# The mLSTM log weights of a two-block transformer kernel: the selected row added in one float32r product instead of a float32 one

## The chip, the cores and the metric

The kernel runs on one core of one Trainium2 chip. The metric is device time in microseconds of the whole program: the median of 3 runs is 2694.84 us (2694.39 to 2695.25).

## What is computed

The program takes 512 tokens and 256 context tokens of width 1024 through two layers of a first block (mLSTM, a gated spatial unit and a convolution side by side, then a gated feed-forward network) and through a second block with two attention mixers. The change lies in the first block's chunked mLSTM. Cut to what matters, the reference does this for each chunk of 128 tokens, each of 4 heads and both directions:

```python
b = jnp.cumsum(fc, axis=-1)
a = b + m[..., None]
Dlog = b[..., :, None] - b[..., None, :] + ic[..., None, :]
Dlog = jnp.where(order, Dlog, -jnp.inf)
m_t = jnp.maximum(a, jnp.max(Dlog, axis=-1))
s = jnp.einsum('bhtk,bhsk->bhts', qc, kc) * jnp.exp(Dlog - m_t[..., None])
```

In the kernel a weight is exp(mask[s, t] + (b - m_t)[t] + (ic - b)[s]). The term in s is a bias per partition of the exponential. The mask and the term in t, the **row** of a head, are what TensorE adds up in PSUM. There are 12 such chunk steps in layer 0 (6 chunks, 2 directions) and 8 in layer 1 (4 chunks, 2 directions), each for 4 heads.

## The kernel before, in words

Everything is written out by hand, engine by engine, with semaphores. Activations lie feature-major. A weight tile of 1024x128 is loaded by SP into a ring of four buffers, split by POOL (`split_weights`, L420 to L427) into an upper part and a rest of type float32r, and multiplied on TensorE as three float32r products (upper times upper, upper times rest, rest times upper). A float32 quantity keeps its accuracy this way with operands of the shorter type. POOL may split tile s when tile s-2 has been used; it waits there on a tiny instruction (L420) for TensorE. In the input projection of the first block the three products are L1508, L1509 and L1510, elsewhere L433, L434 and L436. A tile is 768 columns wide in layer 0 (a pass of 512 and one of 256), and 512 in most of layer 1.

`in_projection` writes TensorE's order by hand. Halves of the projection's tiles 2 to 17 alternate with small pieces of the mLSTM's preparation:

- DVE makes five rows of 8 partitions (4 heads of each direction) over all 768 tokens: `ri` (L2459) is b - m_t. They lie in the memory of `tho`, which is written only later. `columns` (L1467 to L1473) turns two of them, `rb` and `rf`, and the products of `VD` into columns; then DVE copies the identity into `selh` (L2476), an 8 x 8 x 128 selector in float32, computes the arguments `KD` (L2477, L2478) and signals `s_colv`, for which ScalarE's exponentials L1988 and L1989 wait.
- `log_weights(l, i)` (L1476 to L1497) fills one PSUM bank for step i: L1492 is a float32r product, 128 partitions deep and 512 columns wide, of the identity `identr` with the mask; L1495 then adds, for each head, the product of `selh` (8 partitions deep) with 128 columns of `ri`. It uses banks 3 and 4 in turn and waits for ScalarE to have read the bank two steps back (`s_e`).
- ScalarE's `weights(i)` (L1949 to L1960) waits for `s_w` and takes the exponential of the bank, head by head, in 4 instructions (L1959).

The calls of `log_weights` stand behind tile 14 (two), in the middle of tile 15 (two) and behind it (two), in tile 16 (one behind the sums over channels of the convolution, L1503), behind it (two), in tile 17 (one, behind L1503 again) and behind it (two). In layer 1 the last four are empty. After `in_projection` the recurrence begins with `scores` (L1665, which waits for all weights of the layer) in layer 0 and with `update` (L1697) in both.

DVE's further work in this stretch is the convolution (L2311), in portions between its other tasks; in layer 0 it also reads modulation columns (L2269), for which it waits for TensorE (L1391).

Of the kernel before, what the change touches and what calls it, by code (L numbers as in the profile page):

```python
# [14 lines left out]
FP32 = mybir.dt.float32  # L15
FP32R = mybir.dt.float32r
ALU = mybir.AluOpType
# [3 lines left out]
P = 128  # L21
# [3 lines left out]
T = SEQ + CTX  # L25
# [40 lines left out]
def part_start(l, p):  # L66

    return l * LAYER_TILES + N_IN + KT + sum(2 * PARTS[q][1] + KT for q in range(p))
# [40 lines left out]
def mlstm_steps(l):  # L109

    order = ([4, 5, 0, 1, 2, 3], [5, 4, 3, 2, 1, 0])
    return [(d, order[d][i], i == 0, l == 0 or order[d][i] < NX) for i in range(NJ) for d in range(2)] if l < DEPTH else []


def outputs_before(l, t):

    return sum(s[3] for m in range(l) for s in mlstm_steps(m)) + sum(s[3] for s in mlstm_steps(l)[:t])
# [73 lines left out]
def build_program(nc, xT, cT, cb_d, pc_d, fin_d, srow_d, consts_d, sguw_d, wg_d, wmod_d, win_d, wout_d, wgu_d, wdn_d,  # L191
                  b2_d, bmask_d, p_d, wa_d, wao_d, pleg_d, plep_d, wbk_d, wbqz_d, wbo_d, out_d):
    cursor = [nc.sbuf_base + (-nc.sbuf_base) % 64]
    addr_of = {}

    def place(name, shape, dt=FP32, addr=None):
        size = 4
        for s in shape[1:]:
            size *= s
        if addr is None:  # L200
            addr = cursor[0]
            cursor[0] += size + (-size) % 32
        assert addr + size <= nc.sbuf_usable_end, (name, addr + size, nc.sbuf_usable_end)
        addr_of[name] = addr
        return nc.alloc_sbuf_tensor_at(name, shape, dt, offset=addr)

    stack = ExitStack()
    with stack:
# [9 lines left out]
        ident = place("ident", [P, P])  # L218
# [31 lines left out]
        wgl = place("wgl", [P, KT, 16], FP32R)  # L250
        gt = place("gt", [P, NJ, 2, 2, HEADS])
        lf = place("lf", [P, 3, NJ, 8])
        gcol = place("gcol", [P, NJ, 8])
        btm = place("btm", [P, NJ, 8])
        bst = place("bst", [P, NJ, 6])
# [5 lines left out]
        tho = place("tho", [P, HEADS, T])  # L261
# [27 lines left out]

        ri, rf, rb, rm = (place(f"row{i}", [8, T], addr=addr_of["tho"] + i * T * 4) for i in range(4))  # L290
        r2 = place("row4", [8, T], addr=addr_of["vtm"])
        selh = place("selh", [8, 8, P], addr=addr_of["tho"] + 2 * T * 4)
        NUM = [place(f"NUM{e}", [P, HEADS, P + 1], addr=addr_of["YC"] + e * 4 * (HEADS * (P + 1) + 4)) for e in range(2)]
        XF = place("XF", [P, KT, T], addr=addr_of["XH"])
        EP = [place(f"EP{i}", [P, HEADS, P], addr=addr_of["X"] + i * 4 * HEADS * P) for i in range(2 * NJ)]
# [3 lines left out]
        PS = stack.enter_context(nc.psum_tensor("PS", [P, 8, 512], FP32))  # L299
# [114 lines left out]
        def split_weights(pool, s, dyn=0, k=KT):  # L414

            pool.wait_ge(s_raw[s % RING], 16 * (s // RING + 1) + 4 * dyn)
            if s >= 2:
                pool.wait_ge(s_tile, s - 1 + dyn)

            pool.tensor_tensor(word[:, 0:1], ones[:, 0:1], ones[:, 0:1], ALU.mult)  # L420
            for half in range(2):
                ks = slice(half * k // 2, (half + 1) * k // 2)
                src = raw[s % RING][:, 0:k * P].rearrange("p (k c) -> p k c", c=P)[:, ks, :]
                hi, lo = w_hi[s % 2][:, ks, :], w_lo[s % RING][:, ks, :]
                pool.tensor_scalar(hi, src, 1.0, 0.0, ALU.mult, ALU.add).then_inc(s_hi, 1)  # L425
                pool.wait_ge(s_hi, 2 * s + half + 1 + 2 * dyn)
                pool.tensor_tensor(lo, src, hi.bitcast(FP32), ALU.subtract).then_inc(s_split, 1)  # L427
# [894 lines left out]
        @block.gpsimd  # L1322
        def _(pool):
            pool.memset(ones[:], 1.0).then_inc(s_one, 1)
            pool.memset(eps_c[:, 0:1], EPS).then_inc(s_one, 1)
            pool.memset(eps_c[:, 1:2], LN_EPS).then_inc(s_one, 1)
            pool.wait_ge(s_one, 3)
            pool.wait_ge(s_id, 16)
            pool.tensor_scalar(identr[:], ident[:], 1.0, 0.0, ALU.mult, ALU.add).then_inc(s_one, 1)

            for l in range(DEPTH):
                n0 = l * LAYER_TILES
                for n in range(N_IN):
                    split_weights(pool, n0 + n)
                    if l == 0 and n == 3:
                        pool.wait_ge(s_const, 16 * 4)
                        pool.tensor_scalar(mskr[:], mskd[:], 1.0, 0.0, ALU.mult, ALU.add).then_inc(s_one, 1)
                with pool.Fori(0, 2) as i:
                    for u in range(4):
                        split_weights(pool, n0 + N_IN + u, 4 * i)  # L1340
                for p, (h0, hn) in enumerate(PARTS):
                    s = part_start(l, p)
                    with pool.Fori(0, 2 * hn // 4) as i:
                        for u in range(4):
                            split_weights(pool, s + u, 4 * i)
                    with pool.Fori(0, 2) as i:
                        for u in range(4):
                            split_weights(pool, s + 2 * hn + u, 4 * i, hn)
            second_pool(pool)
# [3 lines left out]
        def _(pe):  # L1353
# [121 lines left out]
            def log_weights(l, i):  # L1475

                steps = [s for s in mlstm_steps(l) if s[3]]
                if i >= len(steps):
                    return
                d, j = steps[i][0:2]  # L1480
                o = outputs_before(l, 0) + i
                bank = 3 + i % 2
                if i < 2:
                    pe.wait_ge(s_one, 5)
                    pe.wait_ge(s_mod, 2)
                    pe.wait_ge(s_cole, l + 1)
                    pe.wait_ge(s_mixu, 2 * (l + 1))
                else:
                    pe.wait_ge(s_e, o - 1)
                if i == 0 and l:  # L1490
                    pe.wait_ge(s_tile, l * LAYER_TILES + Q_P)
                pe.matmul(PS[:, bank, :].rearrange("p (h t) -> p h t", h=HEADS), identr[:], mskr[:, d:d + 1, :].to_broadcast([P, HEADS, P]),  # L1492
                          start=True, stop=False)
                for h in range(HEADS):
                    last = pe.matmul(PS[:, bank, h * P:(h + 1) * P], selh[:, 4 * d + h, :], ri[:, j * P:(j + 1) * P],  # L1495
                                     start=False, stop=h == HEADS - 1)
                last.then_inc(s_w, 1)  # L1497

# [56 lines left out]
            def in_projection(l):  # L1555
# [65 lines left out]
                second_half(l, 14)  # L1621
                v_transposed(l, 3)
                log_weights(l, 0)
                log_weights(l, 1)
                first_half(l, 15)
                log_weights(l, 2)
                log_weights(l, 3)
                second_half(l, 15)
# [562 lines left out]
        def _(dve):  # L2191
            links = [0]

            def link(ins):

                links[0] += 1
                ins.then_inc(s_dch, 1)
                dve.wait_ge(s_dch, links[0])
# [15 lines left out]
            def col(l, name, i=0):  # L2214
                return pc[:, l, PC[name] + i:PC[name] + i + 1]
# [132 lines left out]
            for l in range(DEPTH):  # L2348
# [17 lines left out]
                last = dve.tensor_scalar(bcol[:, K_T:V_T], bcol[:, K_T:V_T], K_SCALE, None, ALU.mult)  # L2366
# [56 lines left out]
                for d in range(2):  # L2423
                    last = dve.tensor_scalar(lfv[:, 1, :, d, :], gt[:, :, d, 1, :], 0.0, None, ALU.min)
                link(last)
                link(dve.tensor_tensor(lf[:, 2], lf[:, 1], lf[:, 0], ALU.subtract))
                for d in range(2):
                    last = dve.tensor_copy(lfv[:, 1, :, d, :], gt[:, :, d, 0, :])
# [11 lines left out]
                for r, xs, xc in ((ri, PS[0:8, 3, :], PS[0:8, 4, 0:CTX]), (rf, PS[0:8, 5, :], PS[0:8, 4, CTX:2 * CTX]),  # L2440
                                  (rb, PS[0:8, 6, :], PS[0:8, 7, 0:CTX])):
                    dve.tensor_copy(r[:, ss], xs)
                    last = dve.tensor_copy(r[:, cs], xc)
# [29 lines left out]
                gelu(0)  # L2473
                gelu(1)
                dve.wait_ge(s_cols, l + 1)
                dve.tensor_copy(selh[:], ident[0:8, 0:8].rearrange("p (r c) -> p r c", c=1).to_broadcast([8, 8, P]))  # L2476
                dve.tensor_tensor(KD[:, 0].rearrange("p j e -> p (j e)"), PS[:, 3, 0:8 * NJ], gcol[:].rearrange("p j e -> p (j e)"), ALU.add)  # L2477
                dve.tensor_copy(KD[:, 1].rearrange("p j e -> p (j e)"), PS[:, 3, 8 * NJ:16 * NJ]).then_inc(s_colv, 1)  # L2478
                convolve(l, w, cuts[3], cuts[4])
# [2 lines left out]
                for j in range(nj):  # L2482
                    last = dve.bn_stats(bst[:, j, :], SVT[:, j, :])
                link(last)
                for j in range(nj):
                    last = dve.bn_aggr(bmv[:, j, :], bst[:, j, :])
                last.then_inc(s_svv, 1)
                dve.wait_ge(s_svr, l + 1)
                for j in range(nj):
                    last = dve.tensor_scalar(SVT[:, j, :], SVT[:, j, :], bmv[:, j, 0:1], bmv[:, j, 1:2], ALU.subtract, ALU.mult)  # L2490
                link(last)
                for i in range(2):
                    row = srow[:, 256 * i:256 * (i + 1)].rearrange("p (a c) -> p a c", a=1).to_broadcast([P, nj, 256])
                    last = dve.tensor_tensor(SVT[:, 0:nj, :], SVT[:, 0:nj, :], row, (ALU.mult, ALU.add)[i])
# [16 lines left out]
                for f in range(2):  # L2511
                    last = dve.tensor_tensor(AC[:, f, 0:w], AC[:, f, 0:w], MU[:, 0:w], ALU.subtract)
# [3 lines left out]
                for f in range(2):  # L2516
                    last = dve.scalar_tensor_tensor(out=AC[:, f, 0:w], in0=AC[:, f, 0:w], scalar=col(l, "cg", f), in1=MU[:, 0:w],
                                                    op0=ALU.mult, op1=ALU.mult)
                link(last)
                for f in range(2):  # L2520
                    last = dve.tensor_scalar(AC[:, f, 0:w], AC[:, f, 0:w], col(l, "clb", f), None, ALU.add)
# [269 lines left out]
```

## Time and profile before

| | |
|---|---|
| median of 3 runs | 2694.84 us |
| lowest and highest | 2694.39, 2695.25 us |
| span of the profiled execution | 2693.6 us |
| busy, share of the span | PE 96%, PE weight load 79%, POOL 59%, DVE 52%, ACT 28% |
| data moved | 255.57 MB, mean 95 GB/s |
| chain that ended last | PE 42%, POOL 30%, issue 19%, DVE 5% |

The profiled execution's own time is known by its span, 2693.6 us from the first to the last instruction; the median of the runs is 1.2 us above it. PE is TensorE's matmul side, PEld its weight load, DVE VectorE, ACT ScalarE, POOL GpSimd. PE's busy time is modelled and its matmuls are pipelined, so the start of one to the start of the next tells more than durations do. A float32 product shows as two records of each side, a float32r product as one. The page also gives TensorE's granted clock, as a share of full speed.

### The profile page before, as it was taken

The page shows a single profiled execution, that of the slowest core. Times are in us where ns is not written, and L with a number is a line of the kernel's source. Part 1 is how long each engine was busy: PE and PEld are TensorE (multiplying, and loading weights), DVE is VectorE, ACT ScalarE, POOL GpSimd, SP SyncE. Part 2 cuts the span into 40 slices and gives each one's busy share as a digit, 9 for nine tenths or more (in the row PEclk, how much of TensorE's full clock was granted, in tenths as well). Part 3 has the DMA queues.
Part 4 walks back from the last instruction along what each step waited for, and adds up shares of the span by engine and source line. Part 5 has one row for each costly group of instructions (what it writes and reads, how often), then busy time and mean ns, then how long its engine had stood idle before and what let it go on. Part 6 is the DMA issues. An engine that isn't in the chain of part 4 may idle for free.

```text
span 2693.6 us, 39857 instructions
## 1 busy us (share of the span) xinstructions
PE 2576.0 (96%) x14674; PEld 2116.4 (79%) x14674; DVE 1391.5 (52%) x2054; ACT 754.3 (28%) x1566; POOL 1583.7 (59%) x1668
## 2 busy tenths in 40 slices
PE   5999989999999999999899999999999999899998
PEld 4878978888888886878687877778878887677776
DVE  4862555662662858715533333354454445636744
ACT  3223353211111123234421212222222223324413
POOL 2532224675775665434587777776676765665464
PEclk9999999999999999999999999999999999999999
DMA  6341131332232322111133332433333332222221
GB/s 238 118 156 34 38 152 52 121 123 94 95 126 94 120 86 74 55 50 53 63 95 93 93 94 86 130 106 102 94 95 94 102 102 71 87 89 83 79 94 63
DMA packets 79263, 255.57 MB, mean 95 GB/s; under 512 B 9872, under 2 KB 13712, under 8 KB 78864
## 3 DMA queue, kind: packets, MB, share of 16 engines
q1 hardware_dynamic: 61280, 210.59, 24.3%
q10 hardware_dynamic: 17840, 43.03, 5.3%
q8 instruction: 95, 1.56, 0.2%
q14 instruction: 48, 0.39, 0.1%
HBM read 236.28 MB, written 2.10 MB: 88 GB/s over the span
## 4 chain that ended last, share of the span: by engine, by line
PE 42%; POOL 30%; issue 19%; DVE 5%; DMA 1%; ACT 1%; POOLq 1%; SPq 0%; DVEq 0%; ACTq 0%
POOL w_lo L427 17%; POOL w_hi L425 10%; PE PS L433 8%; PE PS L436 8%; PE PS L434 8%; PE PS L1508 4%; PE PS L1510 4%; PE PS L1509 4%; POOL word L420 2%; PE PS L1495 1%; DVE Z L2230 1%; PE PS L1382 1%; DMA modt<-in_wmod 1%; PE PS L1697 1%; DVE XL L2237 1%
## 5 line engine op out<-in xcount | busy, mean ns | idle before, releaser
L427 POOL TENSOR_TENSOR w_lo<-raw,w_hi 128x512 fp32r<-128x512 f32 (+1 forms) x662 | 957.3, 1446 | 55.2
L433 PE MATMUL PS<-XH,w_hi 128*128 128x512 f32 x2168 | 822.1, 379 | 32.6 <-DVE XL L2595 8.1
L434 PE MATMUL PS<-XL,w_hi 128*128 128x512 f32 x2168 | 794.0, 374 | 0.0
L436 PE MATMUL PS<-XH,w_lo 128*128 128x512 f32 x2168 | 745.0, 375 | 0.0
L420 POOL TENSOR_TENSOR word<-ones 128x1 f32<-128x1 f32 x331 | 103.2, 312 | 1040.4 <-PE PS L436 671.3
L425 POOL TENSOR_SCALAR w_hi<-raw 128x512 fp32r<-128x512 f32 (+1 forms) x662 | 533.4, 806 | 0.0
L433 PEld LDWEIGHTS PS<-XH,w_hi 128*128 128x128 f32 x2168 | 411.4, 190 | 140.9 <-issue 15.1
L434 PEld LDWEIGHTS PS<-XL,w_hi 128*128 128x128 f32 x2168 | 411.6, 190 | 74.1
L436 PEld LDWEIGHTS PS<-XH,w_lo 128*128 128x128 f32 x2168 | 381.4, 190 | 59.4
L1508 PE MATMUL PS<-XH,w_hi 128*128 128x512 f32 (+1 forms) x640 | 235.9, 369 | 10.6 <-DVE XL L2237 10.6
L1509 PE MATMUL PS<-XL,w_hi 128*128 128x512 f32 (+1 forms) x640 | 228.8, 357 | 0.0
L1510 PE MATMUL PS<-XH,w_lo 128*128 128x512 f32 (+1 forms) x640 | 228.7, 357 | 0.0
L2319 DVE TENSOR_TENSOR X<-X,Z 128x768 f32 (+3 forms) x60 | 87.8, 1464 | 226.3 <-ACT Z L1873 221.2
L433 PE MATMUL PS<-HH,w_hi 128*128 128x512 f32 (+1 forms) x528 | 188.4, 357 | 3.4 <-DVE HL L2662 3.4
L434 PE MATMUL PS<-HL,w_hi 128*128 128x512 f32 (+1 forms) x528 | 180.5, 357 | 0.0
L2283 DVE CUSTOM_DVE_ANT_0 cprod<-modv,cb 128x1024 f32<-128x1024 f32 x96 | 165.0, 1719 | 21.2 <-DMA modv<-in_wmod 18.1
L2657 DVE SCALAR_TENSOR_TENSOR Z<-TH,Z 128x768 f32<-128x768 f32 (+1 forms) x44 | 51.4, 1169 | 211.2 <-ACT Z L1854 209.2
L436 PE MATMUL PS<-HH,w_lo 128*128 128x512 f32 (+1 forms) x528 | 159.7, 356 | 0.0
L1508 PEld LDWEIGHTS PS<-XH,w_hi 128*128 128x128 f32 x640 | 125.1, 196 | 31.3 <-issue 11.1
L852 ACT ACTIVATE Z<-PS 128x512 f32<-128x512 f32 x99 | 58.9, 596 | 296.2 <-PE PS L436 292.5
L1510 PEld LDWEIGHTS PS<-XH,w_lo 128*128 128x128 f32 x640 | 124.5, 195 | 17.9
L1509 PEld LDWEIGHTS PS<-XL,w_hi 128*128 128x128 f32 x640 | 125.1, 195 | 15.9 <-issue 0.2
(329 smaller groups left out, 3230.6 us busy)
## 6 DMA issues: line engine op xcount, KB each, us to landing
raw<-in_wgu SPq DMA_DIRECT2D x88, 512.0 KB, 3.5
raw<-in_wa SPq DMA_DIRECT2D x80, 512.0 KB, 3.5
modt<-in_wmod SPq DMA_DIRECT2D x48, 512.0 KB, 9.8
raw<-in_win SPq DMA_DIRECT2D x48, 512.0 KB, 3.6
modv<-in_wmod ACTq DMA_DIRECT2D x48, 512.0 KB, 5.1
raw<-in_wdn SPq DMA_DIRECT2D x32, 512.0 KB, 3.5
QS<-Z ACTq DMA_DIRECT2D x100, 128.0 KB, 2.5
raw<-in_wout SPq DMA_DIRECT2D x16, 512.0 KB, 3.5
```

The source lines that it names most:

```text
L420: pool.tensor_tensor(word[:, 0:1], ones[:, 0:1], ones[:, 0:1], ALU.mult)
L425: pool.tensor_scalar(hi, src, 1.0, 0.0, ALU.mult, ALU.add).then_inc(s_hi, 1)
L427: pool.tensor_tensor(lo, src, hi.bitcast(FP32), ALU.subtract).then_inc(s_split, 1)
L433: pe.matmul(acc(s)[:, a:b], hi, rh[:, i, a:b], start=i == 0, stop=False)
L434: pe.matmul(acc(s)[:, a:b], hi, rl[:, i, a:b], start=False, stop=False)
L436: last = pe.matmul(acc(s)[:, a:b], lo, rh[:, i, a:b], start=False, stop=i == k - 1)
L852: return act.activation(Z[:, n % 4, 0:SEQ], acc(n)[:, 0:SEQ], ACT.Identity)
L1508: pe.matmul(out, hi, XH[:, i, a:b], start=first, stop=False)
L1509: pe.matmul(out, hi, XL[:, i, a:b], start=False, stop=False)
L1510: return pe.matmul(out, lo, XH[:, i, a:b], start=False, stop=i == KT - 1)
L2283: last = dve.tensor_tensor_reduce(out=cprod[:], in0=modv[slots + u][:], in1=cb[:, n, :], scale=0.5, scalar=0.0, op0=ALU.mult, op1=ALU.add, ...
L2319: dve.tensor_tensor(x, x, Z[:, s % 4, 0:w], ALU.add).then_inc(s_used, 1)
```

## The change

The selector `selh` and the float32 product go. In their place stand a float32r operand `RP` of 128 partitions and 768 columns, whose partitions 0 to 7 hold the upper parts of `ri` and whose partitions 32 to 39 hold the rests, the others zero, and a matrix `pick` of 128 x 8 with ones at partitions e and 32 + e of column e. The weights of the product for head e are column e of `pick`, read 128 times with stride zero, so that one product adds upper part and rest of row e to all 128 rows of the output. `pick` is made once by POOL, `RP` once per layer by three DVE instructions where `selh` was copied; it lies where `rf` lay, whose last reader (`columns`) is done by then.

```diff
+        pick = place("pick", [P, 8], FP32R)
...
-        selh = place("selh", [8, 8, P], addr=addr_of["tho"] + 2 * T * 4)
+        RP = place("RP", [P, T], FP32R, addr=addr_of["tho"] + T * 4)
...
             pool.tensor_scalar(identr[:], ident[:], 1.0, 0.0, ALU.mult, ALU.add).then_inc(s_one, 1)
+            pool.tensor_tensor(pick[:], ident[:, 0:8], ident[:, 32:40], ALU.add)
...
                 for h in range(HEADS):
-                    last = pe.matmul(PS[:, bank, h * P:(h + 1) * P], selh[:, 4 * d + h, :], ri[:, j * P:(j + 1) * P],
+                    e = 4 * d + h
+                    last = pe.matmul(PS[:, bank, h * P:(h + 1) * P], pick[:, e:e + 1].to_broadcast([P, P]), RP[:, j * P:(j + 1) * P],
                                      start=False, stop=h == HEADS - 1)
...
                 dve.wait_ge(s_cols, l + 1)
-                dve.tensor_copy(selh[:], ident[0:8, 0:8].rearrange("p (r c) -> p r c", c=1).to_broadcast([8, 8, P]))
+                link(dve.memset(RP[:].bitcast(FP32), 0.0))
+                link(dve.tensor_copy(RP[0:8, :], ri[:]))
+                dve.tensor_tensor(RP[32:40, :], ri[:], RP[0:8, :].bitcast(FP32), ALU.subtract)
                 dve.tensor_tensor(KD[:, 0].rearrange("p j e -> p (j e)"), PS[:, 3, 0:8 * NJ], gcol[:].rearrange("p j e -> p (j e)"), ALU.add)
                 dve.tensor_copy(KD[:, 1].rearrange("p j e -> p (j e)"), PS[:, 3, 8 * NJ:16 * NJ]).then_inc(s_colv, 1)
```

`link` makes DVE wait for the instruction just issued. Every wait, every semaphore and the order of all other work are as before.

VectorE before, in layer 0, where the selector is made (`selh`, `RP`: the operands of the product; `KD`: the arguments of ScalarE's exponentials; `row_180`: `ri`; the first rows are the gated spatial unit's activation, the last the convolution):

```order
L2405 TENSOR_SCALAR Z<-GT 128x768
L2476 COPY selh<-ident 8x1024
L2477 TENSOR_TENSOR KD<-PS,gcol 128x48
L2478 COPY KD<-PS 128x48
L2311 SCALAR_TENSOR_TENSOR AC<-YC,pc,AC 128x8x59
```

and after the change:

```order
L2408 TENSOR_SCALAR Z<-GT 128x768
L2479 MEMSET RP 128x768
L2480 CAST RP<-row_180 8x768
L2481 TENSOR_TENSOR RP<-row_180,RP 8x768
L2482 TENSOR_TENSOR KD<-PS,gcol 128x48
L2483 COPY KD<-PS 128x48
L2314 SCALAR_TENSOR_TENSOR AC<-YC,pc,AC 128x8x59
```

Two instructions more stand ahead of `KD` and of the next portion of the convolution; nothing has moved otherwise.

TensorE before, in layer 0, in the middle of tile 15, where two calls of `log_weights` stand between the tile's pass of 512 columns and its pass of 256:

```order
L1510 MATMUL PS<-XH,w_lo_58 128x512
L1492 MATMUL PS<-mskr,identr 128x512
L1495 MATMUL PS<-row_179,selh 128x128 x4
L1492 MATMUL PS<-mskr,identr 128x512
L1495 MATMUL PS<-row_179,selh 128x128 x4
L1508 MATMUL PS<-XH,w_hi_54 128x256
```

and after the change:

```order
L1513 MATMUL PS<-XH,w_lo_58 128x512
L1494 MATMUL PS<-mskr,identr 128x512
L1498 MATMUL PS<-RP,pick 128x128 x4
L1494 MATMUL PS<-mskr,identr 128x512
L1498 MATMUL PS<-RP,pick 128x128 x4
L1511 MATMUL PS<-XH,w_hi_54 128x256
```

The four products of a call stand in the same place, with other operands.

## Rows read from the trace of the kernel before

**Rows 1.** The page, part 1: busy us, share of the span, instructions

```profile
PE 2576.0 (96%) x14674; PEld 2116.4 (79%) x14674; DVE 1391.5 (52%) x2054; ACT 754.3 (28%) x1566; POOL 1583.7 (59%) x1668
```

**Rows 2.** The chain of waits from 217 to 271 us, by line

```profile
by line: PE PS L1495 24.4%; PE PS L1508 21.3%; PE PS L1510 18.0%; PE PS L1509 17.9%; PE PS L1503 9.6%; PE PS L1492 7.0%; ACT EP L1959 1.2%; PE PS L1398 0.6%; issue 0.5%
```

**Rows 3.** Waits from 1203 us to the end: us in total, times, longest

```profile
POOL word L420 <- PE PS L436: 420.2, 167, 24.3
```

**Rows 4.** TensorE's timeline at tile 15 of layer 0: start us, us

```profile
225.01 0.40 PE L1508 MATMUL PS<-XH,w_hi 128*128 128x512 f32 x1
...
225.71 0.40 PE L1492 MATMUL PS<-mskr,identr 128*128 128x512 f32 x1
226.03 1.15 PE L1495 MATMUL PS<-row,selh 8*128 8x128 f32 x8
227.12 0.51 PE L1492 MATMUL PS<-mskr,identr 128*128 128x512 f32 x1
227.55 1.15 PE L1495 MATMUL PS<-row,selh 8*128 8x128 f32 x8
228.64 0.39 PE L1508 MATMUL PS<-XH,w_hi 128*128 128x256 f32 x1
```

**Rows 5.** The line L1495 alone: ns of one min/median/max, first and last start

```profile
L1495 PE MATMUL PS<-row,selh x160: 270/270/372, 217.4 to 1202.3; 8*128 8x128 f32 x160
```

**Rows 6.** TensorE's timeline after a pair of calls: passes of 256, of 512

```profile
229.09 0.41 PE L1508 MATMUL PS<-XH,w_hi 128*128 128x256 f32 x1
...
229.73 0.41 PE L1508 MATMUL PS<-XH,w_hi 128*128 128x256 f32 x1
...
232.75 0.28 PE L1508 MATMUL PS<-XH,w_hi 128*128 128x256 f32 x1
...
233.10 0.39 PE L1492 MATMUL PS<-mskr,identr 128*128 128x512 f32 x1
...
237.53 0.63 PE L1508 MATMUL PS<-XH,w_hi 128*128 128x512 f32 x1
...
238.81 0.63 PE L1508 MATMUL PS<-XH,w_hi 128*128 128x512 f32 x1
```

**Rows 7.** Stretches: length, busy us (x count) of PE, PEld, DVE, ACT, POOL, granted clock, DMA

```profile
228.50:233.00 4.50, 4.50 (x26) 4.38 (x26) 0.00 (x0) 1.15 (x4) 0.00 (x0) 0.62 0.00 0
...
1184.00:1189.00 5.00, 5.00 (x19) 4.06 (x19) 0.00 (x0) 1.71 (x7) 0.00 (x0) 0.66 0.00 0
283.00:289.00 6.00, 6.00 (x52) 5.91 (x51) 3.22 (x9) 1.28 (x4) 0.00 (x0) 1.00 0.00 0
269.00:278.00 9.00, 7.77 (x43) 7.38 (x43) 4.88 (x6) 5.86 (x17) 3.52 (x3) 0.62 0.14 56
```

**Rows 8.** TensorE's timeline in the recurrence, at 283 us

```profile
283.33 1.05 PE L1697 MATMUL PS<-vtm,Ks 128*128 128x129 f32 x8
```

**Rows 9.** ScalarE's and TensorE's timeline at the end of layer 0's log weights

```profile
267.53 0.69 ACT L1908 ACTIVATE qfm<-PS,bcol 128x512 f32<-128x512 f32 x1 [0.36 <-PE PS L1510]
...
268.76 1.14 ACT L1959 ACTIVATE EP<-PS,gcol 128x128 f32<-128x128 f32 x4 [0.18 <-PE PS L1495]
...
270.34 1.14 ACT L1959 ACTIVATE EP<-PS,gcol 128x128 f32<-128x128 f32 x4 [0.43 <-PE PS L1495]
...
271.54 0.79 PE L1665 MATMUL PS<-qfm,kfm 128*128 128x128 f32 x2 [1.23 <-ACT EP L1959]
```

**Rows 10.** VectorE's selector, its nearest rows, who waits for it, and its idle time

```profile
L2476 DVE COPY selh<-ident x2: 674/678/682, 124.2 to 1105.8; 8x1024 f32<-8x1024 f32 x2
L2637 DVE MEMSET SS<- 128x768 f32 x1 | 0.7, 698 | 0.2 <-DVE cb L2260 0.2
L2461 DVE TENSOR_TENSOR row<-row,mprev x2: 945/946/946, 107.2 to 1094.5; 8x768 f32<-8x768 f32 x2
L1988 ACT ACTIVATE KD<-KD x2: 273/278/282, 131.8 to 1111.6; 128x96 f32<-128x96 f32 x2
DVE bst L2483 <- ACT SVT L1931: 7.4, 1, 7.4
```

## The prediction

> **What bounds the kernel now.** I read the page first: TensorE is busy 96% of the span, no other engine above 59% [rows 1]. A share over the whole span does not say who ends last where the change works, so next comes the chain of waits over 217 to 271 us, the stretch of layer 0 that holds its twelve calls of `log_weights`. It runs on TensorE but for 1.2% on ScalarE; the float32 product L1495 alone is 24.4% of it, the mask's product L1492 7.0% [rows 2]. What these lines give up, the stretch gives up.
>
> Does it reach the end? Behind 1203 us POOL, which splits all weights and stands on the chain as well, waits for TensorE before 167 tiles, 420 us in all [rows 3]. It is paced by TensorE, its loads with it, and the other waits are between neighbours too. A microsecond saved on TensorE moves all that follows.
>
> **What a call costs.** The starts on TensorE's timeline tell it [rows 4]: two calls begin at 225.71 and the next pass at 228.64, so a pair takes 2.93 us, 2.93 to 3.01 in the seven pairs that a pass follows; I take 2.96, or **1.48 us a call**. The mask's product holds 0.41 to 0.43 of it until the first float32 product starts; eight records follow. The line alone has 160 records for 80 products, so each float32 product is two passes [rows 5]. The last lasts 0.37 us, so the eight start (1.15 - 0.37) / 7 = 0.11 us apart: 0.22 a product, and some 0.2 pass before the next kind of product starts.
>
> **What a call will cost.** A float32r product of 512 columns holds TensorE for (225.71 - 225.01) / 3 = 0.233 us [rows 4], one of 256 columns for (233.10 - 232.75) / 3 = 0.117 [rows 6]. None of 128 columns is in the trace. Bounds: by columns, a quarter of 0.233, 0.058; as the two passes of a float32 product of the same shape, 0.22. I take **0.11**: the float32 passes of 128 columns come at this spacing and those of 256 hardly slower, so the weight load of 128 columns seems to set the floor. The two kinds now agree, so the 0.2 us at the change of kind goes. A call is 0.233 + 4 x 0.11 = 0.67, 0.81 less. **20 calls x 0.81 = 16.2 us.** With 0.058 it would be 4.2 more, with 0.22 8.8 less.
>
> The Trainium skill ("TensorE: Matmul & The Clock Gate", Back-to-back issue gap) gives about 81 ns a product for a stream of weight load and 128 columns. The sum by it would be 80 x 0.029 = 2.3 us better, an estimate; the rows here never go below 0.11.
>
> **What ScalarE keeps of it.** In layer 0 the last three calls feed exponentials that stand close together: ScalarE's idle time ahead of the query tile, of step 10 and of step 11 is 0.36 + 0.18 + 0.43 = 0.97 us [rows 9]. TensorE's recurrence starts at 271.54, released by the last of them, after 1.23 us of idle. So these three calls give 0.97 and not 2.4: **1.4 us lost**, and TensorE will wait there some 2.6 us. In layer 1 no call follows the second sum over channels, and ScalarE keeps its distance.
>
> **The clock.** The windows show what the lines cannot. Right behind a pair of calls the granted clock falls from 2.4 to 1.2 GHz: between 228.5 and 233 us its mean is 0.62, between 1184 and 1189 0.66, with TensorE never idle [rows 7]. There are five such stretches, three in layer 0 and two in layer 1, each with 1.70 to 1.71 us of clock missing, (1 - 0.62) x 4.5, or 3.4 us at half speed. What else drops it here is idle time. The pairs are unlike their surroundings in one thing: for 2.2 of 3 us only 8 of the 128 rows of the array work. In the recurrence float32 passes of 128 rows stand 24 in a row and just as close, eight in 1.05 us [rows 8], and the clock stays at 1.00 from 283 to 289 us [rows 7]. So it is the shallow products, I reason, and not float32 or 128 columns that let it fall. The new ones are 128 rows deep and a pair takes 1.35 us. I expect all five stretches to go. At half speed a pass of 256 takes (229.73 - 229.09) / 3 = 0.213 us and one of 512 (238.81 - 237.53) / 3 = 0.427, against 0.117 and 0.233 [rows 4, 6]: 45% of 3.4 us comes back, **5 x 1.55 = 7.8 us**.
>
> **What is added.** DVE zeroes `RP` (0.70 us, by the fill of the same size), then copies and subtracts on 8 x 768 elements (at most 0.95 each, by the nearest row), where it copied the selector in 0.68: 1.9 us more per layer [rows 10]. Behind them on DVE stand the arguments `KD`, two instructions of 0.2 us or less, and the convolution. The selector starts at 124.2 and 1105.8 us, ScalarE takes `KD` at 131.8 and 1111.6 [rows 10]: some 6.7 and 4.9 us of cover, of which 1.9 are used. The convolution is covered by DVE's later waits, 7.4 us for ScalarE in layer 1 [rows 10] and more in layer 0. Cost 0; without that cover, 3.8 us. POOL's sum for `pick` is 8 columns at the program's start, before its first weights have landed: 0.
>
> **The sum.** 16.2 - 1.4 + 7.8 = 22.6 us less. The profiled execution's span of 2693.6 would become 2671.0; from the median of 2694.84, which is 1.2 above it, I get **2672.2 us**.
>
> **Rivals.**
>
> *The clock stays as it is.* The five stretches follow pairs of calls, but not every pair (there is none behind 217 and 1189 us), so the depth of the products may not be what counts; most rows of `RP` are zeros, too. Then the gain is 16.2 - 1.4 = 14.8: 2680.0. Beside it stands a rule of the Trainium skill ("TensorE: Matmul & The Clock Gate", The HAM clock gate): the clock follows how busy TensorE has been, and idle time lowers it. By that rule products issued without a gap should not lower it, and changing their depth should give nothing. Rows 7 speak against it: busy throughout, and half clock. Chance 0.15.
>
> *A sixth stretch goes as well.* From 269 to 278 us the clock is 0.62 over 9 us [rows 7], behind the last pair and the wait for ScalarE. Up to (1 - 0.62) x 9 = 3.4 us would come back: 2669. Against it, the wait grows to 2.6 us. Chance 0.12.
>
> *Narrow float32r is no faster than float32.* At 0.22 a product a call takes 1.11, and 20 save 7.4; ScalarE keeps little of that, the clock gives 7.8: 2680. The same number to a few us covers the change not doing what it says, where the product would be built from two passes. For it: no row has 128 columns. Against it: 256 columns take half of 512, no more. Chance 0.06.
>
> *The saving is caught.* DVE's 3.8 us land on the chain, or a wait behind the stretch absorbs most of it: 2685 to 2690. Rows 3 speak against it. Chance 0.03.
>
> *Slower: weights read with stride zero load slowly.* No weight load in the trace reads one element 128 times. If that cannot stream, each product waits for its weights. It decides from (1.48 - 0.233) / 4 = 0.31 us a product, where a call costs what it did. At 0.43, the slowest spacing of rows 6, a call is 1.95, 20 cost 9.4 more, and the clock is not mended by an array that waits: 2704. Chance 0.02.
>
> **How the numbers follow.** The forecast has 0.62 and is the time predicted. The cases at 2669, 2672 and 2680 hold 0.95 of the chance; the unknown spacing adds 4 below. For 8 in 10 the range reaches from 2667 to 2681. A measurement of this kernel tells about 0.2%, 5.4 us, from no change. Faster by more than that are all cases but the slow one and part of the caught one: 0.96; within it 0.02; slower 0.02.
>
> **What would show it.** L1498 as 80 records, not 160, about 0.11 us apart; pairs of calls of 1.35 us; clock 1.00 over tiles 15 to 17 in both layers, save behind the wait at the recurrence's start; that wait at 2 to 3 us; ScalarE's exponentials of `KD` where they were relative to their tile. It is wrong if pairs take over 2 us, if a stretch of half clock is left inside the tiles, or if `RP` shows up in anybody's wait.

## The result, and the profile after

The changed kernel takes **2661.38 us**, the median of four runs (2659.81 to 2666.65). The kernel before, run on the same chip in turn with it, takes 2695.05 (2694.39 to 2696.39). The measured ratio is 0.9888, with a 95% interval of 0.9877 to 0.9900, which is 30 us; the two medians are 33.7 us apart. The changed kernel is faster by 1.1%, and by more than forecast: 2672.2 had been predicted with a range from 2667 to 2681, and the measured median lies below it. The profiled execution of the changed kernel took 2666.65 us, with a span of 2664.4.

The page of the changed kernel, part 1 (answers to [rows 1]):

```profile
PE 2543.3 (95%) x14594; PEld 2097.1 (79%) x14594; DVE 1401.5 (53%) x2058; ACT 751.6 (28%) x1566; POOL 1579.1 (59%) x1669
```

TensorE has 80 records fewer on each side, VectorE four more, POOL one more: this is the change and nothing else. TensorE is busy 33 us less. VectorE's 10 us more do not repeat: it is busy 1392.1 and 1393.6 us in the two further profiles of this kernel (e1, e10), and what was added to it is 2 x (0.70 + 0.55 + 0.95 - 0.68) = 3.0 us.

The product's line alone in the changed kernel (answers to [rows 5]), with what the engine waited for ahead of it:

```profile
L1498 PEld LDWEIGHTS PS<-RP,pick x80: 187/190/192, 215.4 to 1171.1; 128*128 128x128 f32 x80
L1498 PE MATMUL PS<-RP,pick x80: 219/274/277, 215.7 to 1171.1; 128*128 128x128 f32 x80
its engine sat idle before it (us, times) until:
  issue: 0.2, 1
```

There are 80 records, not 160, and the weight load of stride zero takes 187 to 192 ns: it does stream.

TensorE's timeline of the changed kernel at the same places (answers to [rows 4, 9]): start us, us, and in brackets the idle time ahead.

```profile
215.36 0.48 PE L1494 MATMUL PS<-mskr,identr 128*128 128x512 f32 x1
...
222.39 0.40 PE L1494 MATMUL PS<-mskr,identr 128*128 128x512 f32 x1
222.62 0.56 PE L1498 MATMUL PS<-RP,pick 128*128 128x128 f32 x4
223.01 0.44 PE L1494 MATMUL PS<-mskr,identr 128*128 128x512 f32 x1
223.30 0.56 PE L1498 MATMUL PS<-RP,pick 128*128 128x128 f32 x4
223.69 0.33 PE L1511 MATMUL PS<-XH,w_hi 128*128 128x256 f32 x1
...
256.51 0.38 PE L1668 MATMUL PS<-qfm,kfm 128*128 128x128 f32 x1 [2.11 <-ACT EP L1962]
```

A pair of calls goes from 222.39 to 223.69: 1.30 us, **0.65 a call**, where it was 1.48. Four products take 223.01 - 222.62 = 0.39, or 0.098 each in the mean; in the trace the second starts 0.06 us behind the first and each further one 0.11 behind the one ahead. The wait for ScalarE at the recurrence's start is 2.11 us, where it was 1.23.

Stretches of the changed kernel (answers to [rows 7], the columns are the same: length, busy us of PE, PEld, DVE, ACT, POOL, granted clock, DMA):

```profile
215.00:256.00 41.00, 39.40 (x226) 33.26 (x224) 6.14 (x8) 23.33 (x63) 14.75 (x18) 1.00 0.17 52
256.00:267.00 11.00, 10.40 (x65) 9.16 (x66) 6.47 (x12) 4.20 (x11) 2.65 (x3) 1.00 0.01 1
1150.00:1190.00 40.00, 37.83 (x189) 30.22 (x188) 8.58 (x13) 23.80 (x60) 18.62 (x24) 1.00 0.19 55
```

The clock is 1.00 (2.4 GHz) from the first call to the last, in both layers, and stays there in the recurrence behind them. The same in the kernel before:

```profile
217.00:271.00 54.00, 53.30 (x271) 42.39 (x269) 8.23 (x8) 24.28 (x62) 14.88 (x18) 0.90 0.13 39
271.00:284.00 13.00, 12.46 (x63) 11.41 (x64) 5.58 (x11) 4.29 (x11) 1.52 (x2) 0.77 0.01 2
...
1205.00:1212.00 7.00, 5.06 (x19) 3.14 (x17) 1.91 (x3) 5.43 (x9) 2.26 (x3) 1.00 0.10 21
1212.00:1217.00 5.00, 4.68 (x18) 4.16 (x19) 3.71 (x5) 2.25 (x6) 3.36 (x3) 0.66 0.19 75
```

Where the time went is best seen by cutting TensorE's timeline at the same instructions in every kernel. "Calls 0" goes from the first mask product of layer 0 to the first scores of the recurrence (before: 217.02 to 271.54), "start 0" from there to the second group of `update` that follows (283.33); "calls 1" from the first mask product of layer 1 to the first `update` (1174.45 to 1212.32), "start 1" on to the second group (1217.59). The table has all executions profiled, those of the experiments too; the last column is the measured ratio to the kernel before.

| kernel | calls 0 | start 0 | calls 1 | start 1 | sum | ratio |
|---|---|---|---|---|---|---|
| before | 54.51 | 11.79 | 37.87 | 5.27 | 109.4 | |
| e6_before, the same | 54.49 | 12.06 | 39.29 | 3.77 | 109.6 | 0.9991 |
| e5_dve | 54.47 | 12.09 | 39.32 | 3.75 | 109.6 | 0.9987 |
| e2_shift | 51.42 | 12.06 | 37.81 | 5.36 | 106.7 | 0.9997 |
| **the change** | 41.15 | 9.59 | 28.02 | 3.77 | 82.5 | 0.9888 |
| e1_again, the same | 41.16 | 9.57 | 28.02 | 3.77 | 82.5 | 0.9905 |
| e10_change, the same | 41.15 | 9.60 | 28.02 | 3.76 | 82.5 | 0.9902 |
| e3_deep32 | 45.44 | 9.59 | 31.57 | 3.76 | 90.4 | 0.9923 |
| e4_40deep | 44.19 | 12.12 | 30.71 | 3.77 | 90.8 | 0.9914 |
| e7_shallow_r | 53.88 | 10.72 | 37.35 | 5.36 | 107.3 | 0.9986 |
| e8_last3old | 42.40 | 11.20 | 28.02 | 5.32 | 86.9 | 0.9908 |
| e9_early | 40.63 | 11.75 | 28.02 | 3.77 | 84.2 | 0.9893 |

The change is worth 109.4 - 82.5 = **26.9 us** in these four pieces, and that repeats to 0.1 us in three executions of it. The rest of the difference between two runs lies elsewhere and does not repeat: the two profiles of the kernel before differ by 4.6 us in span and by 0.2 in these pieces. Between the first profiles of the two kernels this rest is 1.7 us ahead of calls 0, 4.3 between start 0 and calls 1, and 3.7 the other way behind start 1. The stretch between start 0 and calls 1 takes 891.1 us before and 886.8 in the change, but also 887.7 in e2 and 886.7 in e7, whose products are 8 rows deep; so it is not the change that shortens it.

### The profile page after: what moved, and what is told of

It is laid out like the page before. It is cut to its first block, busy times and chain, and to the rows that moved or that the text cites. A ratio compares the mean times of both kernels' runs of the same rounds, so it can differ in the third digit from the quotient of the medians.

```text
span 2664.4 us, 39702 instructions
## 1 busy us (share of the span) xinstructions
PE 2543.3 (95%) x14594; PEld 2097.1 (79%) x14594; DVE 1401.5 (53%) x2058; ACT 751.6 (28%) x1566; POOL 1579.1 (59%) x1669
## 4 chain that ended last, share of the span: by engine, by line
PE 42%; POOL 30%; issue 19%; DVE 4%; ACT 1%; DMA 1%; POOLq 1%; SPq 1%; DVEq 0%; ACTq 0%
POOL w_lo L428 17%; POOL w_hi L426 10%; PE PS L434 8%; PE PS L437 8%; PE PS L435 8%; PE PS L1511 4%; PE PS L1512 4%; PE PS L1513 4%; POOL word L421 2%; PE PS L1384 1%; DVE XL L2240 1%; DMA modt<-in_wmod 1%; PE PS L1700 1%; DVE X L1166 1%; DVE Z L2233 1%
## 5 line engine op out<-in xcount | busy, mean ns | idle before, releaser
L2322 DVE TENSOR_TENSOR X<-X,Z 128x768 f32 (+3 forms) x60 | 86.9, 1449 | 223.8 <-ACT Z L1876 218.6
```

The lines of the kernel that those rows point to most:

```text
L2322: dve.tensor_tensor(x, x, Z[:, s % 4, 0:w], ALU.add).then_inc(s_used, 1)
```

## The experiments

**e1_again: the change once more**, in five rounds.

> The change once more, for its interval and a second profile. The first profile shows the stretches of the log weights 22.6 us shorter, as forecast, and the program 29 us shorter (its runs 28 to 35). Theory 'chance downstream': what is beyond 22.6 (the start, one stretch of half clock each behind the recurrence's start, 410, 510 and 2592 us, 6 us lost in mixer B) differs from profile to profile, and the time spreads over several us. Theory 'fixed': the second profile shows the same list and 2659 to 2663 us. Both: 2660 to 2666 us.

Measured: 2663.42 us (2660.64 to 2664.71), before 2690.36 (2686.44 to 2695.12, 15 runs), ratio 0.9905 [0.989, 0.992]. The pieces are those of the first profile. The gain is real and near 26 us; a part of the first 33.7 was the kernel before, which ran 4.7 us quicker here. Outside the pieces the half clock lies where it lay in the first profile up to 2263 us and elsewhere behind that; in e10, a third profile, it differs in more places. So neither theory holds alone: some of these stretches stay where they are and some move.

**e2_shift: the kernel before with the 32 bytes of `pick` taken from the memory**, nothing else.

```diff
+        pick = place("pick", [P, 8], FP32R)
```

> The kernel before with 32 bytes per partition reserved where pick lies, so that all later buffers move as in the change, and nothing else. Theory 'addresses': the slow drift of the gain outside the changed stretches (some 4 us over 1700 us) comes from where buffers lie: 2689 to 2692. Rival: addresses cost nothing: 2694 to 2696.

Measured: 2687.41 us, ratio 0.9997 [0.9988, 1.0006]. What lies behind `pick` in the memory moves by 32 bytes, and that is worth nothing; both times expected were too high, since the kernel before took 2690.36 in this comparison. This execution has 3.1 us less in calls 0 all the same: its clock stayed up behind the calls in tile 15, where it fell in the three other profiles with the calls of the kernel before (before, e5, e6). This execution, then the kernel before:

```profile
227.00:234.00 7.00, 7.00 (x51) 6.15 (x52) 0.00 (x0) 4.10 (x14) 2.63 (x4) 1.00 0.21 72
```

```profile
227.00:234.00 7.00, 7.00 (x41) 6.27 (x40) 0.00 (x0) 2.91 (x10) 0.59 (x2) 0.76 0.00 0
```

So not every pair drops the clock every time. One execution does not tell whether chance or the shift decided it here.

**e3_deep32: 128 rows deep, but float32.**

```diff
-        pick = place("pick", [P, 8], FP32R)
+        pick = place("pick", [P, 8])
...
-        RP = place("RP", [P, T], FP32R, addr=addr_of["tho"] + T * 4)
+        RP = place("RP", [P, T], addr=addr_of["tho"] + T * 4)
...
```

> The change with RP and pick in float32: products 128 rows deep, but in two passes, so a call takes about 1.48 us as before. Theory 'depth': the five stretches of half clock inside the tiles are gone though nothing is quicker: 7.8 us less than before, and with the two at the recurrences' starts 11: 2684 to 2687, with 160 records 0.11 us apart. Rival 'float32 or small products lower the clock': the stretches stay and the time is 2693 to 2696.

Measured: 2667.73 us, ratio 0.9923 [0.9909, 0.9936]. TensorE's timeline of it, and its windows:

```profile
215.52 0.48 PE L1494 MATMUL PS<-mskr,identr 128*128 128x512 f32 x1
215.83 1.05 PE L1498 MATMUL PS<-RP,pick 128*128 128x128 f32 x8
216.64 0.48 PE L1494 MATMUL PS<-mskr,identr 128*128 128x512 f32 x1
216.96 1.05 PE L1498 MATMUL PS<-RP,pick 128*128 128x128 f32 x8
217.77 0.48 PE L1511 MATMUL PS<-XH,w_hi 128*128 128x512 f32 x1
```

```profile
215.00:250.00 35.00, 35.00 (x213) 30.54 (x212) 2.14 (x4) 17.46 (x46) 11.75 (x15) 1.00 0.15 46
261.00:272.00 11.00, 10.91 (x70) 9.67 (x71) 6.01 (x14) 4.01 (x11) 1.82 (x2) 1.00 0.01 2
```

The clock held at 1.00, as expected. The time missed the expectation by some 17 us, because a call takes 1.12 us and not 1.48. The same eight float32 records stand between the same float32r products; what has changed is their depth, and that the weights are read with stride zero, which e7 also has. So the 0.36 us that go belong to the depth, and the change of kind costs nothing that shows: the last record is followed by the next kind after 0.03 us, where it was 0.20. Of the rest, 0.1 us goes ahead of the first record and 0.1 between the first two (0.21 before, 0.11 here). With 0.36 a call and three stretches of 1.55 us, layer 0 should give 12 x 0.36 + 4.65 = 9.0 and gave 54.51 - 45.44 = 9.1; layer 1, 8 x 0.36 + 3.1 = 6.0, gave 6.3.

**e4_40deep: float32r, but 40 rows deep** instead of 128.

```diff
-                    last = pe.matmul(PS[:, bank, h * P:(h + 1) * P], pick[:, e:e + 1].to_broadcast([P, P]), RP[:, j * P:(j + 1) * P],
+                    last = pe.matmul(PS[:, bank, h * P:(h + 1) * P], pick[0:40, e:e + 1].to_broadcast([40, P]), RP[0:40, j * P:(j + 1) * P],
```

> The change with products 40 rows deep (pick and RP cut to partitions 0 to 39), float32r, same sums. Theory 'depth counts, but for as long as it lasts': a pair of calls holds 0.8 us of shallow products, too little to lower the clock: 2660 to 2666 as the change. Rival 'any shallow product lowers it': calls stay at 0.65 us, but stretches of half clock come back: 2668 to 2672.

Measured: 2667.28 us, ratio 0.9914 [0.9898, 0.9929]. TensorE's weight loads and the windows:

```profile
216.97 0.19 PEld L1494 LDWEIGHTS PS<-mskr,identr 128*128 128x128 f32 x1
217.40 0.52 PEld L1498 LDWEIGHTS PS<-RP,pick 40*128 40x128 f32 x4 [0.24 <-issue]
217.99 0.19 PEld L1494 LDWEIGHTS PS<-mskr,identr 128*128 128x128 f32 x1
```

```profile
217.00:255.00 38.00, 38.00 (x191) 29.34 (x190) 2.42 (x3) 17.48 (x48) 11.61 (x15) 1.00 0.13 42
255.00:275.00 20.00, 18.51 (x106) 16.75 (x106) 10.51 (x17) 10.52 (x27) 5.24 (x5) 0.83 0.09 27
```

The calls in pairs take 0.91 to 1.02 us with the same float32r products that take 0.65 at full depth: the cost of leaving the full depth and coming back is there again, about 0.3 us, and the load side shows a part of it as an idle 0.24 us with nothing to wait for. In the tiles the clock stayed at 1.00. The load side is idle for "issue" ahead of all 20 groups, 5.9 us in all, exactly as in e7 and in the kernel before, so this idle time is not what lowers the clock there. Whether it is the 40 rows that keep it up or that the shallow stretch is half as long (four records, not eight), this run does not tell. At the recurrence's start the clock fell again, and start 0 is 12.12 us, that of the kernel before. The median lies just above the 2660 to 2666 expected, since the calls were expected to stay at 0.65.

**e5_dve: the kernel before with VectorE's added work**, whose results nobody reads.

```diff
+        pick = place("pick", [P, 8], FP32R)
...
+        RP = place("RP", [P, T], FP32R, addr=addr_of["tho"] + T * 4)
...
+                link(dve.memset(RP[:].bitcast(FP32), 0.0))
+                link(dve.tensor_copy(RP[0:8, :], ri[:]))
+                dve.tensor_tensor(RP[32:40, :], ri[:], RP[0:8, :].bitcast(FP32), ALU.subtract)
                 dve.tensor_copy(selh[:], ident[0:8, 0:8].rearrange("p (r c) -> p r c", c=1).to_broadcast([8, 8, P]))
```

> The kernel before with the change's three DVE instructions added beside the copy of the selector, and their result used by nobody: 2.3 us more of DVE work per layer. Theory 'covered': same time as before, and ScalarE's exponential of KD starts no later relative to its tile. Rival 'caught': up to 4.6 us slower.

Measured: 2688.3 us, ratio 0.9987 [0.9976, 0.9998], against 0.9991 of the unchanged kernel in the same comparison; the four pieces differ from that kernel's by 0.03 us at most. It is covered.

**e6_before: the kernel before, unchanged**, as a yardstick.

> The kernel before, unchanged, for a second profile. Theory 'the first profile was an unlucky one': half clock behind pairs of calls again, but fewer stretches in all than its 27 units of 3.4 us, elsewhere than before (none at 31 us, one fewer at 500), and a span of 2684 to 2692. Rival: the same list and 2693 to 2695.

Measured: 2689.37 us (2684.52 to 2700.3, 10 runs), ratio 0.9991 [0.998, 1.0003]. Its windows behind pairs of calls:

```profile
229.00:241.00 12.00, 12.00 (x60) 10.32 (x60) 0.00 (x0) 5.11 (x17) 3.90 (x5) 0.72 0.14 44
1178.00:1198.00 20.00, 20.00 (x81) 15.48 (x80) 0.00 (x0) 6.93 (x24) 5.42 (x7) 0.74 0.10 32
```

The stretches of half clock are there as in the first profile. In layer 1 a third one, which had stood at the recurrence's start (start 1, 5.27 us), lies among the calls here (3.77 us, and calls 1 longer by 1.4). The profiled execution was not quicker than the first one, as I had expected, but slower (span 2698.2), while the median was lower by 5. The kernel before scatters over 16 us.

**e7_shallow_r: float32r, eight rows deep, twice.** Each product becomes two of 8 partitions of `pick` and `RP`, so that the count of records, 160, is that of the kernel before. It adds the upper parts twice and leaves the rests out, so what it computes is not the kernel's result.

```diff
-                    last = pe.matmul(PS[:, bank, h * P:(h + 1) * P], pick[:, e:e + 1].to_broadcast([P, P]), RP[:, j * P:(j + 1) * P],
-                                     start=False, stop=h == HEADS - 1)
+                    for b in range(2):
+                        last = pe.matmul(PS[:, bank, h * P:(h + 1) * P], pick[0:8, e:e + 1].to_broadcast([8, P]), RP[0:8, j * P:(j + 1) * P],
+                                         start=False, stop=h == HEADS - 1 and b == 1)
```

> The change with each product replaced by two float32r products of partitions 0 to 7 alone. It adds the upper parts of the row twice and leaves the rests out. Float32r as in the change, shallow and as long as before: 160 passes 0.11 us apart. Theory 'depth': calls of 1.45 to 1.5 us, half clock behind pairs as before, 2687 to 2695. Rival 'float32 lowers the clock': no stretches inside tiles, 2675 to 2680.

Measured: 2686.26 us, ratio 0.9986 [0.9975, 0.9997]. The line alone, and windows behind two pairs:

```profile
L1499 PE MATMUL PS<-RP,pick x160: 267/269/323, 216.7 to 1195.0; 8*128 8x128 f32 x160
its engine sat idle before it (us, times) until:
  issue: 5.9, 20
```

```profile
228.00:233.00 5.00, 5.00 (x30) 4.71 (x28) 0.00 (x0) 1.54 (x6) 0.58 (x2) 0.66 0.00 0
235.00:240.00 5.00, 5.00 (x16) 3.95 (x16) 0.00 (x0) 1.14 (x4) 1.42 (x2) 0.66 0.03 12
```

For the clock this is the clean one of the set: the type and the stride-zero weights of the change, the depth and the count of the kernel before, and the clock falls to half behind the pairs. The calls in pairs take 1.36 to 1.46 us; the weight-load side, not the matmul side, idles 5.9 us ahead of the 20 groups, 0.30 each, for "issue". Nearly all of the gain is gone, in part because there are eight products a call and not four: it is e3, with as many records at full depth, that it is to be compared with, 1.12 us a call. Together with e3 it separates the two: float32 at full depth keeps the clock, float32r at eight rows loses it. The median lies 0.7 us below the 2687 to 2695 expected.

**e8_last3old: the change, with the last three calls of layer 0 as before.**

```diff
+        selh = place("selh", [8, 8, P], addr=addr_of["tho"] + 2 * T * 4)
...
                     e = 4 * d + h
+                    if i >= 9:
+                        last = pe.matmul(PS[:, bank, h * P:(h + 1) * P], selh[:, e, :], ri[:, j * P:(j + 1) * P],
+                                         start=False, stop=h == HEADS - 1)
+                        continue
...
+                dve.tensor_copy(selh[:], ident[0:8, 0:8].rearrange("p (r c) -> p r c", c=1).to_broadcast([8, 8, P]))
```

> The change, but the last three calls of layer 0 keep the shallow float32 products (layer 1 has no such calls). Theory 'shallow products also set the clock at the recurrence': half clock comes back at the start of layer 0's recurrence (two units, 3 us), the calls cost 1 us: 2664 to 2667, stage 217 to 280 some 4 us longer than in the change. Rival 'the wait for ScalarE sets it': no half clock there, 1 us longer.

Measured: 2667.27 us, ratio 0.9908 [0.9888, 0.9928]. Its windows, the calls up to the ninth and the recurrence's start:

```profile
216.00:250.00 34.00, 34.00 (x187) 28.33 (x185) 1.84 (x3) 16.67 (x46) 11.81 (x15) 1.00 0.16 47
257.00:270.00 13.00, 11.68 (x62) 10.24 (x61) 6.52 (x12) 5.02 (x14) 2.68 (x3) 0.87 0.05 19
```

With three old calls the half clock at the recurrence's start is back, and start 0 grows from 9.59 to 11.20; with the 1.25 us of the calls that is 2.9 us, where some 4 had been expected. In layer 1 no old call is left, and start 1 is at 5.32, the long value, as well: half clock can come there without them. So the link between these three calls and the clock behind them does not rest on this run alone, but on 9.57 to 9.60 in four executions without shallow products (the change three times and e3) against 10.72 to 12.12 in seven with them. (The 11.75 of e9 below is another thing, waits at full clock.)

**e9_early: the change with calls 9 and 10, and ScalarE's exponentials for them, ahead of the convolution's second sum**, to see whether the wait of 2.1 us can be had too. On TensorE, and likewise on ScalarE:

```diff
+                log_weights(l, 9)
+                log_weights(l, 10)
                 pe.wait_ge(s_csq, l + 1)
                 conv_sum(l, YC, s_cvar)
-                log_weights(l, 9)
                 second_half(l, 17)
-                log_weights(l, 10)
                 log_weights(l, 11)
```

> The change, with steps 9 and 10 of layer 0's log weights moved ahead of the second sum over channels of the convolution, on TensorE and on ScalarE, where ScalarE idles 3.6 us. Theory 'ScalarE's last exponentials set the recurrence's start': its wait of 2.1 us falls to nearly nothing and the stretch from the first mask product to the first scores takes 39 to 39.5 us, not 41.15; in the whole, 2 us, less than the time spreads. Rival: something else is as late there (the query tile's evacuation, VectorE): the stretch stays over 40.5 us.

Measured: 2663.66 us, ratio 0.9893 [0.9877, 0.9908]. The waits of TensorE at the recurrence's start, and ScalarE's timeline ahead of it:

```profile
PE PS L1668 <- DVE EP L2559: 1.9, 1, 1.9
PE PS L1668 <- ACT EP L1962: 1.8, 1, 1.8
```

```profile
250.49 2.18 ACT L1962 ACTIVATE EP<-PS,gcol 128x128 f32<-128x128 f32 x8 [2.97 <-PE PS L1498]
252.68 1.28 ACT L1811 ACT_TABLE_LOAD   x1
...
256.19 0.85 ACT L1812 ACTIVATE MU<-MU 128x768 f32<-128x768 f32 x1
257.87 1.14 ACT L1962 ACTIVATE EP<-PS,gcol 128x128 f32<-128x128 f32 x4
```

A miss, and the rival held: calls 0 became shorter by 0.5 us and not by 1.6 to 2 (40.63 us, over the 40.5 named), and start 0 longer by 2.2. The two exponentials, 2.18 us, now stand ahead of the convolution's root (L1811 to L1812), so that the root is finished later, the last exponential stands behind it at 257.87, and TensorE waits 1.8 us for it. Then a wait of 1.9 us for VectorE opens. The work was only put in another order on an engine that is itself the last here.

**e10_change: the change a third time**, beside e9.

> The change beside it on the same chip. Theory: what the change gives is what its two stages give, 26.9 us, and the rest is chance: 24 to 30 us less than before in the comparison, both stages as in its two earlier profiles within 0.1 us (41.15 and 28.02 us) though the span may differ by several us.

Measured: 2668.04 us (2660.45 to 2669.65), ratio 0.9902 [0.9884, 0.9919]. So e9 is no faster than the change within what can be told, and no version run here beats it.

## Why the prediction was right in its parts and wrong in its time

**What bounds the kernel: right.** The calls' savings reached the end of the program; nothing behind them took them back. The four pieces give 26.9 us, and the three comparisons of the change give 2691 times 1 minus the ratio, or 30, 26 and 26 us.

**What a call costs and will cost: right in size, wrong in one reason.** Predicted 0.67 us, measured 0.65, so that 20 calls save 16.6 and not 16.2. But "so the 0.2 us at the change of kind goes" is wrong. Of the old 1.48 us, 1.12 are what the same records take at full depth (e3) and 0.36 the change between 128 rows and 8. e3 has both kinds side by side and loses nothing; e7 has one kind and two depths and loses 0.3. The number came out because the same edit removed both, which is luck. A reading was off as well: the mask's product was said to hold 0.41 to 0.43 us until the first float32 product, but in the rows shown it is 226.03 - 225.71 = 0.32 for the first call of a pair; nothing was worked out from it.

The Trainium skill ("TensorE: Matmul & The Clock Gate", Back-to-back issue gap) had about 81 ns a product for such a stream. The trace does not reach it: it shows 98 in the mean, one spacing of 0.06 us and then 0.11 between products, which is the 110 predicted. Over 80 products the mean is 1 us better than the sum had it.

**What ScalarE keeps of it: right.** Layer 0's calls and clock should have given 12 x 0.83 + 3 x 1.55 = 14.6 and gave 54.51 - 41.15 = 13.4: 1.2 us were lost, where 1.4 was predicted. In layer 1, where nothing was to be lost, 8 x 0.83 + 2 x 1.55 = 9.7 stand against 9.9. The wait is 2.11 us, not 2.6.

**The clock in the tiles: right.** All five stretches went, in all three executions. The two stages of calls together gave 13.4 + 9.9 = 23.2 us, where 22.6 was the whole forecast. Its reason, that it is the shallow products and not float32 or 128 columns, is what e3 and e7 show.

The rule of the Trainium skill that was weighed there ("TensorE: Matmul & The Clock Gate", The HAM clock gate), by which a busy TensorE keeps its clock, does not hold for products of eight rows: in e7 the matmul side is busy 5.00 of 5.00 us at a clock of 0.66, and it does not idle in the pair ahead either. The measurement decides.

**What is added: right.** VectorE's three instructions take 0.70 + 0.55 + 0.95 us, and e5 shows them covered. ScalarE takes `KD` 7.4 and 5.6 us behind the first of them, where it was 7.6 and 5.8 behind the selector's copy, and nobody waits for these three. Stride-zero weights load in 187 to 192 ns: that rival is out.

**The step that failed** is "What else drops it here is idle time". On it the forecast left the half clock at the recurrence's starts alone. In layer 0 it had been seen and given as a rival of 0.12, "a sixth stretch goes as well"; in layer 1 the list of "two in layer 1" overlooked the stretch at 1212 us altogether (0.66 above), since it lies behind a wait and not behind a pair. The runs show both gone, although the wait in layer 0 grew from 1.23 to 2.11 us: start 0 went from 11.79 to 9.59 and start 1 from 5.27 to 3.77, **3.7 us**. An idle time of 2 us alone does not lower the clock there, nor did e9's two waits of 1.8 and 1.9 us; with shallow products ahead of it the clock was low in all seven executions of layer 0 that have them (8 or 40 rows). In layer 1 the third stretch lies now at the start (before, e2, e7), now among the calls (e5, e6), but the five executions with 8-row products all have three over both pieces, and of the seven without them e8 alone has one. So 1.5 of the 3.7 us are tied to the depth less strictly than the rest.

That step accounts for 3.7 of the 10.8 us between 2672.2 and 2661.4; the calls add 0.4 and what ScalarE keeps of them 0.2. The other 6.5 us lie outside the four pieces. With 26.9 us in place of 22.6 the sum would have given 2667.9, just inside the range, so the second fault was needed for the miss as well.

**The base was the second fault.** The sum was set against 2694.84, the median of three runs that lay within 0.9 us, and the range treated the kernel's own scatter as nothing. In 25, 15 and 9 further runs, in three later comparisons, it went from 2686.3 to 2699.6, from 2686.4 to 2695.1 and from 2686.9 to 2695.6, with medians of 2692.32, 2690.36 and 2691.55. These were on several chips, and how much of the difference is the chip's and how much chance, the runs do not tell. From 2691, 26.9 us less is 2664, in the middle of the change's three medians, 2661.4, 2663.4 and 2668.0. What scatters is partly the clock in places that the change does not touch. From 20 to 50 us the mean clock of the first profile and of e6_before, which are one kernel, is 0.83 and 0.72, and the second reaches its first mask product 1.2 us later (218.27 against 217.02):

```profile
20.00:50.00 30.00, 16.54 (x264) 13.79 (x256) 13.58 (x22) 10.08 (x17) 8.79 (x10) 0.83 0.69 272
```

```profile
20.00:50.00 30.00, 19.28 (x260) 16.09 (x252) 13.49 (x22) 10.08 (x17) 9.25 (x10) 0.72 0.70 274
```

**What stays open.** Why 40 rows hold the clock in the tiles but did not at the recurrence's start was seen in one execution and not tried again. Which of the pairs drops the clock differs between two executions of the kernel before itself (in layer 1, before and e6), and what decides it was not found. Nor was a product of 8 rows tried in stretches as short as e4's, so that depth and length of the shallow stretch are not told apart.

## What to carry to other kernels

Read the granted clock beside the timeline, and when a stretch of half clock has no idle time ahead of it, look at how many rows of the array the products ahead of it use; deepening them with zero rows can cost nothing and give the clock back, behind the next wait too. Count the spacing at each change of depth as a cost of its own: few, full-depth products beat many shallow ones twice. And take the base and its scatter from more than three runs before a range of half a per cent is set.

## What was not expected of the hardware

- Leaving the full depth and coming back costs 0.3 to 0.36 us a group, whatever the type: 1.48 against 1.12 us a call for float32 (8 and 128 rows), about 0.97 against 0.65 for float32r (40 and 128 rows). The weight loads themselves take as long at any depth, 180 to 186 ns for 8 rows in e7 and 187 to 192 for 128.
- Float32r products of 128 columns stand 0.11 us apart in a group (0.098 in the mean of four, since the second comes after 0.06), of 256 columns 0.117, of 512 0.233: a product of 128 columns saves nearly nothing against one of 256.
- Products of 8 rows lower the clock from 2.4 to 1.2 GHz with TensorE's matmul side busy all the time (e7: 0.66 over 5.00 us, busy 5.00), and the drop can lie behind the wait that follows them (0.77 from 271 to 284 us before, 1.00 in the change).
